# Relative-position buckets of the second block: compared in the expert loop with two bounds, not made ahead by 15 comparisons

## The chip, the cores and the metric

The kernel runs on one core of one Trainium2 chip. The metric is the device time of one execution in microseconds (us), lower is better. Engines are named as in the profile: PE is TensorE, DVE is VectorE, ACT is ScalarE, POOL is GpSimd, SP is the queue engine that issues most DMAs.

## What is computed

Two transformer blocks run one after the other on 256 tokens of width 1024, in float32.

- The first block has an adaptive norm, two attentions of 8 heads each, and a mixture of 32 experts of which each token takes 4.
- The second block has a gated feed-forward, a mixer (a Fourier branch and a differential attention of 4 heads), and a second feed-forward.

The change concerns the bias of the second block's attention. For each query and key the signed distance of their positions picks one of 32 buckets, and the bucket picks a value for each head:

```
rel = positions[key] - positions[query]
bucket = 16 * (rel > 0) + (|rel| if |rel| < 8 else a logarithmic step up to 15)
scores[head, query, key] += rel_bias[bucket, head]
```

The steps of |rel| at which the bucket goes up by one are 15 numbers, `TWO_SIDED = [1, 2, ..., 8, 12, 16, 23, 32, 46, 64, 91]`.

## The kernel before, in words

All of it is one program with hand-written instruction streams for SP, POOL, ACT, PE and DVE that meet at semaphores. On DVE the helper `link` makes an operation count up a semaphore and waits for it at once, so that the next one may read what it wrote.

**Opening and first projection.** SP streams weight slabs of 4 MB into a ring of four slots. In the order of the stream these are two slabs of the adaptive norm, three of `w_in`, one more of the norm, and so on; a slab is loaded once the last user of its slot is done (L573, `release`). Each projection is made of pieces. ACT copies a piece to a high part (`split_until`, L735), DVE subtracts to get the low part (`split_until`, L1622, the operation is L1630), and PE multiplies (L1042 to L1044). `copy_units` on DVE (L1652) makes these low parts and copies results out of PSUM.

**The buckets.** At the very start DVE makes the signed distances of all 256 x 256 pairs (`distances`, L1792) as a tile `REL` of 128 x 512. Then it turns them into buckets: three operations (L1806 to L1808) make the absolute value and the 16 of the positive side, and `buckets` (L1810) adds one comparison per step, each over 128 x 512 elements and each through the helper `stt` (L1618). Six comparisons come before the first norm (L1855), and three stand after each of the first three pairs of projection units (L1857 to L1859). ACT waits for them before the first attention (L891). POOL waits too, and copies the result to the tile `BK` after the attention has used its space (L690, L691).

**The expert loop.** SP loads each expert's 12 MB in six parts of 2 MB (L547). There are nine places for parts, and a part waits until PE has used the one nine before it. PE gathers the tokens of each expert in chunks of 32, multiplies (L1354), turns the gates (L1382), gathers for the next expert (L1336), multiplies down (L1411) and adds into the totals (L1421). DVE runs a loop of 4 passes over 8 unrolled experts (L2038). For each expert e it makes the gates of e (L2012), the row selector (L1790) and the selection (L1947) for e+1, the products of e once PE's gate and up products are there (L2024 to L2034), and the gathered tokens of e+1 (L2006). Last in the body it makes the part of the position bias that belongs to bucket e: a mask `BKM` where the bucket equals e (L2054), and for each of four heads `BIAS2 += BKM * value` (L2057 to L2060, through L1618). So the 32 buckets are spread over the 32 experts.

**After the loop** comes the post-norm of the first block (L1759 on DVE), then the second block. Its attention reads `BIAS2` in two parts (L2089 to L2094).

Of the kernel before, what the change touches and what calls it, by code (L numbers as in the profile page):

```python
# [23 lines left out]
ALU = mybir.AluOpType  # L24
# [3 lines left out]
P = 128  # L28
T = 256
# [6 lines left out]
NE = 32  # L36
# [20 lines left out]
CAUSAL_BUCKETS = [1, 2, 3, 4, 5, 6, 7, 8, 9, 10, 11, 12, 13, 14, 15, 16, 19, 21, 24, 27, 31, 35, 40, 46, 52,  # L57
                  59, 67, 77, 87, 99, 113]

C_ID, C_FLIP, C_MASK, C_TRI, C_OH, C_IOTA, C_END = 0, 128, 256, 384, 896, 1152, 1280  # L60

R_C, R_GPM, R_GPF, R_F1, R_MN, R_F2, R_ADA, R_SUB, R_END = 0, 8, 16, 24, 32, 40, 48, 96, 97

# [1 line left out]
def tables():  # L65

    k = np.zeros((P, C_END), np.float32)
    i = np.arange(P)
    k[:, C_ID:C_ID + P] = i[:, None] == i[None, :]
    k[:, C_FLIP:C_FLIP + P] = i[:, None] == P - 1 - i[None, :]  # L70
    k[:, C_MASK:C_MASK + P] = np.where(i[None, :] > i[:, None], NEG, 0.0)
    t = np.arange(T)
    for tt in range(TT):
        k[:, C_TRI + tt * T:C_TRI + (tt + 1) * T] = (tt * P + i)[:, None] <= t[None, :]
    bucket = np.searchsorted(CAUSAL_BUCKETS, T - 1 - t, side="right")
    k[:NE, C_OH:C_OH + T] = np.arange(NE)[:, None] == bucket[None, :]
    k[:, C_IOTA:C_IOTA + P] = i
    f = np.zeros((P, 5 * T), np.float32)
    for st in range(TT):
        a = 2 * np.pi * ((st * P + i)[:, None] * t[None, :] % T) / T  # L80
        f[:, st * 2 * T:st * 2 * T + T] = np.cos(a)
        f[:, st * 2 * T + T:(st + 1) * 2 * T] = np.sin(a)
    b = 2 * np.pi * (i[:, None] * i[None, :] % P) / P
    f[:, 4 * T:4 * T + P] = np.cos(b) / math.sqrt(T * P)
    f[:, 4 * T + P:5 * T] = -np.sin(b) / math.sqrt(T * P)
    return k, f


def two_blocks(nc, a, const1, const2, out):
    with ExitStack() as ctx:  # L90
        def sb(name, cols, parts=P, dt=F32):
            return ctx.enter_context(nc.sbuf_tensor(name, [parts, cols], dt))
# [27 lines left out]
        HTf, arena = rows_and_arena[:, 0:KT * T], rows_and_arena[:, KT * T:KT * T + ARENA_COLS]  # L120
        HT = HTf.rearrange("p (k t) -> p k t", k=KT)
        K1 = sb("ident", P)
        IOTA = sb("iota", P)
        ONES = sb("ones", P)
        VALS = sb("vals", 32 * 4)
        VC = sb("veccols", 104)
# [86 lines left out]
        NP = T + TT  # L213
        POS_RAW, POS_HI, POS_LO = (HTf[:, 260 * j:260 * j + NP].bitcast(I32) for j in range(3))
        POS_HF, POS_LF = (HTf[:, 780 + 260 * j:780 + 260 * j + NP] for j in range(2))
        REL, BKX = area(13272, TT, T), area(14808, TT, T)
        RTMP = HTf[:, 0:TT * T].rearrange("p (a b) -> p a b", a=TT)

        GS = area(4096, KT, T)
        HH = part("hidden_high", arena_at, 6144, FT * T)[:, :].rearrange("p (k t) -> p k t", k=FT)  # L220
# [415 lines left out]
        def _(pool):  # L636
# [50 lines left out]

            gate_rows(1, 5, "g_post_ffn")
            pool.wait_ge(sem("att_turned"), NHEAD // 2)
            pool.wait_ge(sem("buckets"), 1)  # L690
            link(pool.tensor_copy(BK, BKX))  # L691
            pool.sem_inc(sem("pool_kept"), 1)
            link(pool.memset(BIAS2, 0.0))
            pool.sem_inc(sem("pool_kept"), 1)
# [13 lines left out]
        def _(act):  # L708
# [7 lines left out]
            load(K1[:, :], const1[:, C_ID:C_ID + P], "k_in")  # L716
            load(OH, const1[0:NE, C_OH:C_OH + T], "oh_in")
            load(RB1, a["rel_bias"], "oh_in")
            load(IOTA[:, :], const1[:, C_IOTA:C_IOTA + P], "tri_in")
            load(TRI, const1[:, C_TRI:C_TRI + 2 * T].rearrange("p (t n) -> p t n", t=TT), "tri_in")  # L720

            def f(out_, in_, func=ACT.Copy, **kw):
# [165 lines left out]
                act.wait_ge(sem("att_mixed"), j + 1)  # L888
                f(MIXH[:, j, :], PS[:, MIX_BANK[j], 0:T]).then_inc(sem("mix_high"), 1)

            act.wait_ge(sem("buckets"), 1)  # L891
            split_at = {3: 0, 5: 2, 6: 3}
            for p in range(NHEAD // 2 + 1):
                if p == NHEAD // 2:
# [713 lines left out]
        def _(dve):  # L1608
# [183 lines left out]
            def distances():  # L1792

                dve.wait_ge(sem("pos_in"), 32)
                v.tensor_scalar(POS_HI, POS_RAW, 16, None, ALU.arith_shift_right)
                link(v.tensor_scalar(POS_LO, POS_RAW, 65535, None, ALU.bitwise_and))
                v.tensor_copy(POS_HF, POS_HI)
                link(v.tensor_copy(POS_LF, POS_LO))
                for tt in range(TT):
                    ins = v.tensor_scalar(REL[:, tt, :], POS_HF[:, 0:T], POS_HF[:, T + tt:T + tt + 1], 65536.0,  # L1800
                                          ALU.subtract, ALU.mult)
                link(ins)
                for tt in range(TT):
                    ins = stt(REL[:, tt, :], POS_LF[:, 0:T], POS_LF[:, T + tt:T + tt + 1], REL[:, tt, :], ALU.subtract, ALU.add)
                link(ins)
                link(v.tensor_scalar(BKX, REL, 0.0, 16.0, ALU.is_gt, ALU.mult))  # L1806
                link(v.tensor_scalar(RTMP, BKX, 0.125, -1.0, ALU.mult, ALU.add))
                link(v.tensor_tensor(REL, REL, RTMP, ALU.mult))  # L1808

            def buckets(n0, n1):  # L1810
                for step_at in TWO_SIDED[n0:n1]:
                    link(stt(BKX, REL, float(step_at), BKX, ALU.is_ge, ALU.add))

            def ada_row(part, n):

# [36 lines left out]
            link(v.tensor_scalar(ST[:, 73:74], VC[:, R_SUB:R_SUB + 1], 1.0 - LAMBDA_INIT, None, ALU.mult))  # L1852
            dve.wait_ge(sem("curve_A"), 1)
            v.tensor_tensor(COND[:, :], COND[:, :], VC[:, 0:8], ALU.mult).then_inc(sem("opening_D"), 1)
            buckets(0, 6)  # L1855
            norm(0, AB[:, 8:16], AB[:, 0:8])
            for n in range(3):  # L1857
                copy_units(m0[0] + 2 * n, m0[0] + 2 * n + 2)
                buckets(6 + 3 * n, 9 + 3 * n)  # L1859
            dve.sem_inc(sem("buckets"), 1)  # L1860
            dve.wait_ge(sem("trow_out"), 16)
            v.tensor_copy(ID_R, ident)
            dve.wait_ge(sem("mask_in"), 32)
# [174 lines left out]
            with dve.Fori(0, NE // DVE_TURN) as i:  # L2038
                for q in range(DVE_TURN):
# [10 lines left out]
                    chunks(dve, n_next, e + 1, spread((q + 1) % 2), [sem("xt_sb")])  # L2050

                    dve.wait_ge(sem("pool_kept"), 2)
                    dve.wait_ge(sem("bias2"), e * 2 + 1)
                    v.tensor_scalar(BKM, BK.rearrange("p a b -> p (a b)"), IOTA[:, bass.ds(e, 1)], None,  # L2054
                                    ALU.is_equal).then_inc(sem("bias2"), 1)
                    dve.wait_ge(sem("bias2"), e * 2 + 2)
                    for h in range(4):  # L2057
                        acc = BIAS2[:, h, :, :].rearrange("p a b -> p (a b)")
                        ins = stt(acc, BKM, VALS[:, bass.ds(e * 4 + h, 1)], acc, ALU.mult, ALU.add)
# [147 lines left out]
```

## Time and profile before

| | us |
|---|---|
| median of 3 runs | 1714.8 |
| lowest and highest of them | 1712.97, 1719.04 |
| span of the profiled execution | 1709.8 |
| PE busy in it | 1466.4 (86%) |
| DVE busy in it | 769.3 (45%) |
| ACT busy in it | 463.4 (27%) |
| POOL busy in it | 24.1 (1%) |

The span runs from the first to the last instruction of one profiled execution. The page gives no further time of that execution, so the span is the time of its own that the working is made against; the median of the runs lies 5.0 us above it. The rows are read this way: the number before an engine is a time within the span or a duration in us, what stands in square brackets is how long the engine had been idle just before and what it was waiting for, and "xN" is the number of instructions.

### The profile page before, as it was taken

How to read it: one execution, taken by the hardware profiler on the slowest of the kernel's cores; microseconds unless marked ns; L12 is line 12 of the kernel's file. 1: busy time of each engine (PE TensorE's matmuls, PEld its weight loads, DVE VectorE, ACT ScalarE, POOL GpSimd, SP SyncE). 2: the span in 40 equal slices, each digit the busy share in tenths (PEclk: the TensorE clock that was granted, in tenths of full speed). 3: DMA queues.
4: the chain of work that ended last, by engine and by line, in shares of the span. 5: the costliest groups of instructions: out<-in, count | busy, mean ns of one | idle time of the engine just before them, and what ended most of it. 6: DMA issues, size and time to landing. Idle time of an engine off the chain costs nothing. (4 is left out here: it accounts for less than half of the span.)

```text
span 1709.8 us, 26362 instructions
## 1 busy us (share of the span) xinstructions
PE 1466.4 (86%) x10243; PEld 847.9 (50%) x10243; DVE 769.3 (45%) x1447; ACT 463.4 (27%) x881; POOL 24.1 (1%) x48
## 2 busy tenths in 40 slices
PE   4999888887898999779977665759999999999998
PEld 3977522322232333213322111228888877988887
DVE  4776532332242332323332221337775647767764
ACT  2535310000010010000100000026554537556553
POOL 2002000000000000000000000000000000000000
PEclk9999999999899999889999898889999999999999
DMA  9878799999999999999999999982454742505460
GB/s 349 317 273 334 283 386 424 426 425 424 427 425 427 426 423 405 425 426 426 425 427 425 425 425 426 426 344 102 173 209 194 288 162 90 192 28 197 164 255 25
DMA packets 69011, 549.32 MB, mean 321 GB/s; under 512 B 6001, under 2 KB 6778, under 8 KB 44250
## 3 DMA queue, kind: packets, MB, share of 16 engines
q1 hardware_dynamic: 66392, 542.67, 77.1%
q0 software_dynamic: 1744, 3.53, 0.6%
q8 instruction: 138, 2.26, 0.5%
q10 hardware_dynamic: 690, 0.48, 0.1%
q14 instruction: 47, 0.39, 0.1%
HBM read 545.59 MB, written 1.07 MB: 320 GB/s over the span
## 5 line engine op out<-in xcount | busy, mean ns | idle before, releaser
L1354 PE MATMUL PS<-ring,arena 128*32 128x512 f32 x2768 | 342.4, 633 | 87.1 <-DMA ring<-in_w_gate_up 83.0
L1630 DVE TENSOR_TENSOR weights_low<-ring,weights_high 128x1024 fp32r<-128x1024 f32 x212 | 257.7, 1220 | 86.0 <-ACT weights_high L723 86.0
L1048 PE MATMUL PS<-ht_pair,weights_high 128*128 128x512 f32 x832 | 291.9, 396 | 3.9 <-DVE weights_low L1630 2.6
L2024 DVE TENSOR_SCALAR arena<-PS 128x256 f32<-128x256 f32 x47 | 19.9, 424 | 529.7 <-PE PS L1354 529.7
L723 ACT ACTIVATE weights_high<-ring 128x1024 fp32r<-128x1024 f32 x212 | 222.6, 1056 | 97.1 <-PE PS L1044 97.0
L723 ACT ACTIVATE arena<-PS 128x256 f32<-128x256 f32 (+2 forms) x237 | 100.6, 432 | 516.8 <-PE PS L1411 343.1
L1354 PEld LDWEIGHTS PS<-ring,arena 128*32 128x32 f32 x2768 | 84.4, 113 | 314.8 <-issue 186.3
L1050 PE MATMUL PS<-ht_pair,weights_low 128*128 128x256 f32 x832 | 232.0, 279 | 0.0
L1048 PEld LDWEIGHTS PS<-ht_pair,weights_high 128*128 128x128 f32 x832 | 156.1, 188 | 41.9 <-issue 4.8
L723 ACT ACTIVATE arena<-arena 128x256 f32<-128x256 f32 (+2 forms) x113 | 45.7, 405 | 451.7 <-DVE arena L2024 447.4
L1050 PEld LDWEIGHTS PS<-ht_pair,weights_low 128*128 128x128 f32 x832 | 156.7, 188 | 0.0
L1411 PE MATMUL PS<-ring,arena 128*32 128x512 f32 x1264 | 144.4, 594 | 13.2 <-PEq L492 11.5
L1421 PE MATMUL PS<-arena 64*128 64x512 f32 x384 | 104.3, 673 | 8.6 <-PEq L492 7.9
L1411 PEld LDWEIGHTS PS<-ring,arena 128*32 128x32 f32 x1264 | 44.8, 109 | 112.1 <-issue 106.4
L1618 DVE SCALAR_TENSOR_TENSOR arena<-arena,vals 128x512 f32<-128x512 f32 x128 | 87.7, 748 | 5.9 <-DVE arena L2054 2.1
L1336 PE MATMUL PS<-XN,arena 128*32 128x256 f32 x768 | 57.5, 435 | 21.3 <-ACTq L492 18.6
L1421 PEld LDWEIGHTS PS<-arena 64*128 64x128 f32 x384 | 41.5, 207 | 59.5 <-issue 57.8
L1042 PE MATMUL PS<-weights_high,hidden_high 128*128 128x512 f32 x176 | 68.5, 389 | 0.0
L1044 PE MATMUL PS<-weights_high,hidden_low 128*128 128x512 f32 x176 | 68.5, 389 | 0.0
L1043 PE MATMUL PS<-weights_low,hidden_high 128*128 128x512 f32 x176 | 68.5, 389 | 0.0
L1043 PE MATMUL PS<-ht_pair,weights_high 128*128 128x256 f32 x192 | 54.3, 283 | 0.0
L1667 DVE TENSOR_TENSOR arena<-PS,arena 128x256 f32<-128x256 f32 x60 | 25.4, 424 | 58.0 <-ACT arena L723 57.8
(292 smaller groups left out, 1637.2 us busy)
## 6 DMA issues: line engine op xcount, KB each, us to landing
ring<-in_w_gate_up SPq DMA_DIRECT2D x117, 2048.0 KB, 33.7
ring<-in_w_down SPq DMA_DIRECT2D x54, 2048.0 KB, 35.5
ring<-in_w_ada SPq DMA_DIRECT2D x6, 4096.0 KB, 16.2
ring<-in_w_in SPq DMA_DIRECT2D x6, 4096.0 KB, 13.9
arena<-in_w_gate_up SPq DMA_DIRECT2D x11, 2048.0 KB, 35.4
arena<-in_w_down SPq DMA_DIRECT2D x10, 2048.0 KB, 35.5
ring<-in_ffn_wg SPq DMA_DIRECT2D x4, 4096.0 KB, 13.3
ring<-in_ffn_wu SPq DMA_DIRECT2D x4, 4096.0 KB, 13.6
```

The source lines that it names most:

```text
L723: return nc.scalar.activation(out_, in_, func, **kw)
L1042: mm(out_, lhs[0], rhs[0], start=first, stop=False, **kw)
L1043: mm(out_, lhs[0], rhs[1], start=False, stop=False, **kw)
L1044: return mm(out_, lhs[1], rhs[0], start=False, stop=last, **kw)
L1048: mm(PS[:, bank, :].rearrange("p (a t) -> p a t", a=2), high, HT_PAIR[:, :, k, :], start=first, stop=False, skip_group_check=True)
L1050: return mm(PS[:, bank, 0:T], low, HT_PAIR[:, 0, k, :], start=False, stop=last, skip_group_check=True)
L1336: ins = mm(PS[CH * t:CH * (t + 1), ROW_BANK[c % INL], 0:QC], SEL[:, tt, o:o + CH], XN[:, tt, t * QC:(t + 1) * QC], start=tt == 0, stop=tt ...
L1354: ins = mm(PS[CH * t:CH * (t + 1), c % INL, :].rearrange("p (u n) -> p u n", u=2), XTE[b][c % INL][:, KT // 2 * half + k, :], w[:, k % 2, ...
L1411: ins = mm(PS[CH * g:CH * (g + 1), DOWN_BANK[c % INL], :], HID[c % INL][:, k + j, :], w[:, k % 4 + j, h * HALF:(h + 1) * HALF], start=k == ...
L1421: ins = mm(total(tt, h), SGT[b][c % INL][r, tt * P:(tt + 1) * P], YS[c % INL][r, :], start=False, stop=False, skip_group_check=True)
L1618: return v.scalar_tensor_tensor(out=out_, in0=in0, scalar=scalar, in1=in1, op0=op0, op1=op1)
L1630: v.tensor_tensor(low, w, high, ALU.subtract).then_inc(sem("split_low"), 1)
```

## The change

The opening still makes the signed distances, but nothing of the absolute value, of the 16 for the positive side, or of the 15 comparisons. The signed distances go to the place where the buckets were (offset 14808), and POOL copies them to `BK` at the same point. ACT's wait at L891 is gone. Two small tables, 32 lower bounds and 32 upper bounds, are added to the constant table and come with the `IOTA` load, which grows from 128 to 192 columns. In the expert loop the one comparison with the bucket number becomes two: distance at least the lower bound of bucket e, then distance at most its upper bound, multiplied into the mask.

```diff
-C_ID, C_FLIP, C_MASK, C_TRI, C_OH, C_IOTA, C_END = 0, 128, 256, 384, 896, 1152, 1280
+C_ID, C_FLIP, C_MASK, C_TRI, C_OH, C_IOTA, C_LEAST, C_MOST, C_END = 0, 128, 256, 384, 896, 1152, 1280, 1312, 1344
...
+    edges = [0, *TWO_SIDED, 1e30]
+    for n in range(NE // 2):
+        k[:, C_LEAST + n], k[:, C_MOST + n] = 1 - edges[n + 1], -edges[n]
+        k[:, C_LEAST + NE // 2 + n], k[:, C_MOST + NE // 2 + n] = max(1, edges[n]), edges[n + 1] - 1
...
-        IOTA = sb("iota", P)
+        IOTA = sb("iota", P + 2 * NE)
...
-        REL, BKX = area(13272, TT, T), area(14808, TT, T)
-        RTMP = HTf[:, 0:TT * T].rearrange("p (a b) -> p a b", a=TT)
+        REL = area(14808, TT, T)
...
-            pool.wait_ge(sem("buckets"), 1)
-            link(pool.tensor_copy(BK, BKX))
+            pool.wait_ge(sem("distances"), 1)
+            link(pool.tensor_copy(BK, REL))
...
-            load(IOTA[:, :], const1[:, C_IOTA:C_IOTA + P], "tri_in")
+            load(IOTA[:, :], const1[:, C_IOTA:C_END], "tri_in")
...
-            act.wait_ge(sem("buckets"), 1)
...
-                link(ins)
-                link(v.tensor_scalar(BKX, REL, 0.0, 16.0, ALU.is_gt, ALU.mult))
-                link(v.tensor_scalar(RTMP, BKX, 0.125, -1.0, ALU.mult, ALU.add))
-                link(v.tensor_tensor(REL, REL, RTMP, ALU.mult))
-
-            def buckets(n0, n1):
-                for step_at in TWO_SIDED[n0:n1]:
-                    link(stt(BKX, REL, float(step_at), BKX, ALU.is_ge, ALU.add))
+                ins.then_inc(sem("distances"), 1)
...
-            buckets(0, 6)
             norm(0, AB[:, 8:16], AB[:, 0:8])
-            for n in range(3):
-                copy_units(m0[0] + 2 * n, m0[0] + 2 * n + 2)
-                buckets(6 + 3 * n, 9 + 3 * n)
-            dve.sem_inc(sem("buckets"), 1)
+            copy_units(m0[0], FORGET)
...
-                    dve.wait_ge(sem("bias2"), e * 2 + 1)
-                    v.tensor_scalar(BKM, BK.rearrange("p a b -> p (a b)"), IOTA[:, bass.ds(e, 1)], None,
-                                    ALU.is_equal).then_inc(sem("bias2"), 1)
-                    dve.wait_ge(sem("bias2"), e * 2 + 2)
+                    away = BK.rearrange("p a b -> p (a b)")
+                    dve.wait_ge(sem("bias2"), e * 3 + 1)
+                    v.tensor_scalar(BKM, away, IOTA[:, bass.ds(e + P, 1)], None, ALU.is_ge).then_inc(sem("bias2"), 1)
+                    dve.wait_ge(sem("bias2"), e * 3 + 2)
+                    stt(BKM, away, IOTA[:, bass.ds(e + P + NE, 1)], BKM, ALU.is_le, ALU.mult).then_inc(sem("bias2"), 1)
+                    dve.wait_ge(sem("bias2"), e * 3 + 3)
```

## Rows read from the trace of the kernel before

**Rows 1.** Busy time by engine in the two halves of the expert loop
```profile
223.00:700.00 477.00, 408.82 (x3350) 137.90 (x3346) 154.35 (x354) 39.93 (x85) 0.00 (x0) 0.97 1.00 422
700.00:1138.00 438.00, 318.81 (x2326) 95.86 (x2318) 118.76 (x267) 26.71 (x57) 0.00 (x0) 0.90 1.00 421
```

**Rows 2.** DMA of 223 to 1130 us: GB/s in 40 equal slices
```profile
GB/s 385 428 425 424 426 426 427 423 425 425 427 426 425 426 427 426 426 421 395 418 425 423 425 427 425 426 425 425 426 425 426 425 426 426 425 425 426 426 426 404
```

**Rows 3.** Waits of PE, 230 to 1140 us: total us, times, longest
```profile
PE PS L1354 <- DMA ring<-in_w_gate_up: 83.0, 40, 3.9
...
PE PS L1344 <- DVE expert_rows L1790: 0.7, 1, 0.7
```

**Rows 4.** PE busy, sum over eight windows that cover 43.6 to 113.2 us
```profile
sum 69.60, PE 69.58; mean PE 8.70
```

**Rows 5.** PE groups, 43.5 to 113.2 us: the one with idle time
```profile
L1042 PE MATMUL PS<-ht_high,weights_high 128*128 128x256 f32 x128 | 36.5, 285 | 0.4 <-DVE weights_low L1630 0.4
```

**Rows 6.** DVE groups by shape, 9 to 66 us: busy us, mean ns
```profile
L1618 DVE SCALAR_TENSOR_TENSOR arena<-arena 128x512 f32<-128x512 f32 x15 | 10.3, 690 | 0.4
...
L1808 DVE TENSOR_TENSOR arena<-arena 128x512 f32<-128x512 f32 x1 | 0.7, 693 | 0.0
...
L1806 DVE TENSOR_SCALAR arena<-arena 128x512 f32<-128x512 f32 x1 | 0.4, 429 | 0.0
```

**Rows 7.** DVE timeline, before the first norm: start us, us
```profile
13.86 0.26 DVE L1842 COPY veccols<-PS 128x97 f32<-128x97 f32 x1 [0.21 <-PE PS L1173]
...
16.43 4.32 DVE L1618 SCALAR_TENSOR_TENSOR arena<-arena 128x512 f32<-128x512 f32 x6
21.29 0.15 DVE L1696 TENSOR_SCALAR stats<-stats 128x1 f32<-128x1 f32 x1 [0.54 <-ACT XN L723]
```

**Rows 8.** DVE timeline, in the first projection
```profile
55.74 2.14 DVE L1618 SCALAR_TENSOR_TENSOR arena<-arena 128x512 f32<-128x512 f32 x3
57.91 1.22 DVE L1630 TENSOR_TENSOR weights_low<-ring,weights_high 128x1024 fp32r<-128x1024 f32 x1
...
67.63 2.44 DVE L1630 TENSOR_TENSOR weights_low<-ring,weights_high 128x1024 fp32r<-128x1024 f32 x2 [0.77 <-ACT weights_high L723]
```

**Rows 9.** SP timeline: two loads of the adaptive norm's weights
```profile
59.16 22.36 SPq L582 DMA_DIRECT2D ring<-in_w_ada  x2
```

**Rows 10.** PE timeline: the first products of the first value piece
```profile
67.15 0.40 PE L1042 MATMUL PS<-weights_high,ht_high 128*128 128x512 f32 x1
67.39 0.40 PE L1043 MATMUL PS<-weights_low,ht_high 128*128 128x512 f32 x1
```

**Rows 11.** DVE groups by shape, 222 to 1140 us: busy, mean ns, idle before
```profile
L1618 DVE SCALAR_TENSOR_TENSOR arena<-arena,vals 128x512 f32<-128x512 f32 x128 | 87.7, 748 | 5.9 <-DVE arena L2054 2.1
...
L2012 DVE TENSOR_SCALAR arena<-iota,arena 128x128 f32<-128x128 f32 x90 | 25.8, 343 | 19.4 <-issue 12.9 <-PE PS L1421 4.9 <-PEq L492 1.5
...
L2024 DVE TENSOR_SCALAR arena<-PS 128x256 f32<-128x256 f32 x46 | 19.5, 424 | 521.2 <-PE PS L1354 521.2
...
L2054 DVE TENSOR_SCALAR arena<-arena,iota 128x512 f32<-128x512 f32 x32 | 15.6, 487 | 11.6 <-DVEq L492 11.6
```

**Rows 12.** DVE timeline: the shortest idle time before an expert's first product
```profile
683.94 0.43 DVE L2024 TENSOR_SCALAR arena<-PS 128x256 f32<-128x256 f32 x1 [7.55 <-PE PS L1354]
```

**Rows 13.** Timeline of DVE and PE at the end of the expert loop
```profile
1134.27 0.49 DVE L2054 TENSOR_SCALAR arena<-arena,iota 128x512 f32<-128x512 f32 x1 [0.35 <-DVEq L492]
1134.89 2.74 DVE L1618 SCALAR_TENSOR_TENSOR arena<-arena,vals 128x512 f32<-128x512 f32 x4
...
1143.22 0.69 DVE L1759 TENSOR_TENSOR XN<-PS,arena 128x512 f32<-128x512 f32 x1 [5.59 <-PEq L492]
...
1150.09 2.50 PE L1056 MATMUL PS<-ident 128*128 128x128 f32 x10 [7.08 <-issue]
...
1150.68 0.88 DVE L1708 TENSOR_SCALAR XN<-X,stats 128x512 f32<-128x512 f32 x2
...
1152.39 1.87 PE L1130 MATMUL PS<-ident,XN 128*128 128x128 f32 x8
```

## The prediction

> **What bounds the kernel now.** I read the times by stage first. In the two halves of the expert loop DVE works 154 of 477 us and 119 of 438 us, PE is granted 0.97 and 0.90 of its clock, and the DMA share is 1.00 with 422 and 421 GB/s [rows 1]. The DMA view of the same stretch shows 425 GB/s in nearly every slice [rows 2]. So from 223 to 1138 us, over half of the span, the weight stream sets the time: its end is its start plus its bytes over its rate. PE's waits agree. It waits 83.0 us for gate-up weights, and for a result of DVE it waits once, 0.7 us [rows 3].
>
> The change moves DVE work from the opening into this loop, so the second question is who bounds the opening, where the comparisons are taken away. The PE windows from 43.6 to 113.2 us add up to 69.58 busy of 69.60 us [rows 4], at full clock, and the one group of products with idle time before it has 0.4 us, at the start of the stretch [rows 5]. PE bounds the first projection, and it is never late for want of DVE inside it. Nine of the fifteen comparisons lie in that stretch. The other six lie before the first norm, beside the arrival of X.
>
> **What the change removes.** Fifteen comparisons of 0.690 us are 10.3 us of DVE; of the three operations before them L1806 has 0.429 and L1808 0.693 [rows 6], and L1807, alike to L1806, about the same as it, so together 1.6 us. In all 11.9 us of DVE time. Where each part stood:
>
> - The three operations before the comparisons end before 13.86 us, and there DVE still waits 0.21 us for a transpose of PE [rows 7]. PE had that from a DMA, not from DVE. Worth: nothing.
> - Six comparisons take 4.32 us from 16.43, so 0.72 each from start to start. Behind them stands the mean of the squares, which starts at 21.29 after 0.54 us of waiting for ACT's sum over X [rows 7]. Without them DVE waits 4.9 us in place of 0.54. The cover is the load of X and ACT's squares; if it were gone, this part would give 4.3 us. Worth: nothing.
> - Nine comparisons, three after each of three pairs of units, take 2.14 us a time, 6.4 us in all [rows 8]. Each delays the low part of the next piece. The plainest case: the split at 57.91 starts the moment the comparisons of 55.74 end [rows 8], so it would come up to 2.1 us earlier. PE does not wait for it [rows 4, 5].
> - The tightest cover is at the change to the value units. PE starts the first value piece at 67.15 with 0.24 us a product [rows 10]; a piece has 12 products, so the next is wanted at 67.15 + 12 x 0.23 = 69.9. Its low part is the first of the two splits that start at 67.63 [rows 8], done about 68.85. That is 1.1 us in hand now, and about 3 without the comparisons. Worth: nothing.
> - The split that ends at 59.13 frees the slot into which SP issues the adaptive norm's third slab at 59.16 [rows 8, 9]. That load starts up to 2 us earlier. The next one on SP waits for PE-paced pieces again (the two take 22.36 us to issue [rows 9]), so the expert stream behind it does not start earlier. Worth: nothing, at most 2 us if the whole stream shifted with it.
> - ACT's wait before the attention and POOL's before its copy are long met: the comparisons end near 64 us, and the first attention follows the last product at 113. Nothing.
>
> **What it adds.** Per expert one more two-tensor operation over 128 x 512. The nearest row is the bias sum of the same line, shape and kind of operand (a scalar per partition, picked by a register): 0.748 us [rows 11]. The comparisons of the opening, with a constant as scalar, are the lower bound, 0.690 [rows 6]. To this comes the gap of a linked operation, 0.14 us from the end at 1134.76 to the start at 1134.89 [rows 13], and perhaps register work for one more address and one more wait value: the mask operation has 11.6 us of that over 32, 0.36 each [rows 11]. So 0.83 to 1.25 us an expert; I take 0.89, since the mask's 0.36 follows other waits and the sum that reads VALS through a register has only the gap. The comparison that stays keeps its form and its 0.487 us. Sum: 32 x 0.89 = 28.5 us of DVE (27 to 40). DVE busy goes from 769.3 to 769.3 - 11.9 + 32 x 0.748 = 781.3 us.
>
> What hides it: the bias is the last thing in the body. Behind it on DVE are the gates of the next expert, its row selector and selection (PE wants all three only after the next gate-up products), then the first product of the next expert, which waits for PE. That wait is 521.2 us in all [rows 11], and before the first product of an expert the shortest is 7.55 us [rows 12]. 1.25 us goes into 7.55 six times. Worth in the loop: nothing. ACT and SP wait for nothing that comes after the bias.
>
> The last expert has no next one. Its bias ends at 1134.89 + 2.74 = 1137.63, and DVE then waits until 1143.22, 5.59 us, for PE's last sum [rows 13]. Even if DVE came late there, PE itself is away for 7.08 us and transposes the normed rows at 1152.39, while DVE has the first half of them at 1150.68 + 0.44 = 1151.12 [rows 13], another 1.2 us in hand. Nothing.
>
> The IOTA load grows from 512 to 768 B a row, 32 KB more, at under 10 us, and nothing reads it before the router. The copy on POOL stays as it is. Nothing.
>
> **A rule against the change.** The trace has, before the gates at three of the loop's turns, idle time with no releaser, 12.9 us together, so 4.3 each [rows 11], and PE has 7.08 us of the same kind where it leaves the expert code [rows 13]. DVE too must skip the code of the crowded case there, inside its 5.59 us, and how much of that the skip takes no row shows. The Trainium skill (Runtime: NRT & Kernel Launch, Instruction fetch mechanics) says that a taken branch out of the pages at hand makes the engine fetch before it goes on. By that rule a body that is longer by eight operations with their register work can only add such stalls; the trace agrees that they exist. What it would give is the third rival.
>
> The sum on the path: 0 removed, 0 added. On the profiled span that is 1709.8 us again, and 5.0 us above it, as before, the median: 1714.8.
>
> **The rivals.**
>
> 1. *The opening was bound by DVE after all* (faster). PE's ends are modelled, so small waits could be hidden in "busy". If the nine comparisons were all exposed: 1714.8 - 6.4 = 1708.4; with the six and the three as well, 1714.8 - 12.3 = 1702.5. Against it: 69.58 of 69.60 us, and products that follow each other at an even pace [rows 4, 10]. For it: only that the splits do start at the end of the comparisons [rows 8]. The one way to a real gain is the earlier load, up to 2 us. Chance of over 0.3%: 0.09.
>
> 2. *DVE becomes the bound of the expert loop* (slower). The place is the next expert's gates, which PE wants right after its gate-up products. It decides from the point where the idle time before an expert's first product is under 1 us. Then each expert is 0.89 longer: 1714.8 + 28.5 = 1743.3. Against it: the shortest such idle time is 7.55 us [rows 12], and the DMA stream would swallow delays of PE anyway. For it: nothing but that DVE's part grows. Chance 0.03.
>
> 3. *Longer code costs a fetch where it is not covered* (inside 0.3% or just over). If DVE's 5.59 us at the loop's end were wholly used by its own skip, the added 1.25 and one more stall of 4.3 would show, less the 1.2 us of PE: 1714.8 + 4.4 = 1719.2. A stall inside the loop is covered by 7.55 us. Chance 0.07, of which about half over 0.3%.
>
> 4. *Another cause of slower*, above all the DMA rate, since nearly a whole stage hangs on it: 0.3% of it would be 3 us. Chance of over 0.3%: 0.04.
>
> That the change does not do what it says I see no way for: the four steps are plain operations.
>
> **How the numbers follow.** The forecast is no change, 1714.8, chance 0.77; with the part of rival 3 within the bound, "same" gets 0.80, "faster" 0.09 and "slower" 0.03 + 0.04 + 0.04 = 0.11. A measurement of this kernel can tell about 0.3%, 5.1 us, from no change; the three runs lie 6.1 us apart. The range has the scatter of such a median, some 3 us either side, beyond it the 2 us of the earlier load and most of rival 1's first case below, and rival 3's 4.4 us above: 1709 to 1720. Rival 2 and the full case of rival 1 are left out.
>
> **What would show it.** In the profile after: (a) L1618 over 128 x 512 without VALS in the opening gone, and DVE idle 4.9 us before L1696; (b) PE from 43.6 to 113.2 as full as now, first product within 0.2 us of 43.6; (c) the low part of the second value piece done by 67.5 rather than 68.9; (d) 32 new operations near 0.75 us, the time from the mask's start to the end of the sums 4.25 in place of 3.36 us; (e) DVE's wait before the first product 0.9 us shorter per expert, some 490 us in all, nowhere under 6; (f) DMA at 1.00 and 425 GB/s throughout, PE leaving the loop within 2 us of 1143. I am wrong if the first projection is shorter by microseconds (rival 1), if PE waits for DVE at L1382 or L1336 (rival 2), or if DVE's post-norm starts well after PE's last sum (rival 3).

## The result: 3.9 us slower, and where the time went

| | before | after |
|---|---|---|
| median, us | 1715.53 (20 runs) | 1719.83 (20 runs) |
| lowest to highest | 1711.12 to 1721.48 | 1716.28 to 1724.59 |
| span of the profiled execution | 1709.8 | 1716.7 |
| PE busy / DVE busy in it | 1466.4 / 769.3 | 1467.7 / 781.4 |

The ratio after to before is 1.0023, interval 1.0013 to 1.0033. By it the change costs 3.9 us (2.2 to 5.7); the two medians lie 4.3 us apart. That is less than the 0.3% that the prediction called detectable, but with twenty runs of each it is clear of the scatter. The forecast of no change was wrong. The median of 1719.83 does lie inside the stated range of 1709 to 1720, but only at its edge, and only because the range had been widened for rival 3.

Most of the profile looks like the forecast. First the opening, in the timeline of DVE in the kernel after (start us, duration us, and idle time before with its releaser in brackets):

```profile
15.96 0.17 DVE L1849 TENSOR_TENSOR cond<-cond,veccols 128x8 f32<-128x8 f32 x1
21.40 0.15 DVE L1698 TENSOR_SCALAR stats<-stats 128x1 f32<-128x1 f32 x1 [5.28 <-ACT XN L726]
...
65.73 2.45 DVE L1632 TENSOR_TENSOR weights_low<-ring,weights_high 128x1024 fp32r<-128x1024 f32 x2 [0.77 <-ACT weights_high L726]
```

Without the six comparisons DVE waits 5.28 us for ACT where it waited 0.54, and starts its next step 0.11 us later than before [rows 7]. The first low part of the value units is done at about 66.95 in place of 68.85 [rows 8]. Neither shortens anything: PE's first projection is as full as before.

Then the groups of DVE in the expert loop, with busy us, mean ns and idle time before:

```profile
L1620 DVE SCALAR_TENSOR_TENSOR arena<-arena,vals 128x512 f32<-128x512 f32 x127 | 87.0, 747 | 4.6 <-DVE arena L1620 0.2
L2003 DVE TENSOR_SCALAR arena<-iota,arena 128x128 f32<-128x128 f32 x90 | 25.8, 343 | 14.9 <-issue 12.9 <-PE PS L1423 1.5 <-PEq L495 0.5
L1620 DVE SCALAR_TENSOR_TENSOR arena<-arena,iota 128x512 f32<-128x512 f32 x32 | 24.0, 752 | 4.7 <-DVE arena L2046 1.8
L2015 DVE TENSOR_SCALAR arena<-PS 128x256 f32<-128x256 f32 x47 | 19.9, 424 | 507.7 <-PE PS L1356 507.7
L2046 DVE TENSOR_SCALAR arena<-arena,iota 128x512 f32<-128x512 f32 x32 | 15.6, 486 | 12.6 <-DVEq L495 12.6
L1792 DVE CAST expert_rows<-arena 128x128 fp32r x31 | 7.0, 227 | 19.5 <-DVEq L495 19.5
```

The 32 new operations take 752 ns each. The wait before an expert's first product falls from 521.2 to 507.7 us in all [rows 11] (8.35 of the 507.7 is the first expert's wait, which the row before does not hold), and from the second expert on its shortest at an expert's start is 9.62 us, so DVE is in nobody's way. One row has more than doubled: before the row selector (L1792, L1790 in the kernel before) DVE was idle for 19.5 us in all, where it was 8.6. The chain of waits below shows what that is.

The windows of the opening and the loop (PE, PEld, DVE, ACT, POOL busy us with counts, then granted clock, DMA share, GB/s), kernel after:

```profile
43.60:113.20 69.60, 69.20 (x488) 64.70 (x488) 45.68 (x52) 28.44 (x36) 0.00 (x0) 1.00 0.68 268
113.20:223.00 109.80, 100.82 (x809) 67.36 (x811) 62.68 (x162) 46.74 (x133) 13.48 (x23) 0.95 0.82 318
223.00:700.00 477.00, 408.68 (x3362) 137.76 (x3354) 167.16 (x372) 40.95 (x87) 0.00 (x0) 0.97 0.99 419
700.00:1138.00 438.00, 314.89 (x2280) 92.61 (x2280) 123.09 (x270) 25.92 (x55) 0.00 (x0) 0.88 1.00 423
```

PE fills the first projection as before (it starts it at 44.00 us in place of 43.62; the missing 0.4 us is that start), and DMA runs at the same share as in [rows 1] once the loop is under way. The waits and the loop's end do not look alike, though. PE's waits from 230 to 1140 us, and its timeline where it leaves the loop, kernel after:

```profile
PE PS L1356 <- DMA ring<-in_w_gate_up: 91.0, 43, 4.1
...
PE PS L1346 <- DVE expert_rows L1792: 0.5, 1, 0.5
```

```profile
1149.32 1.99 PE L1423 MATMUL PS<-arena 64*128 64x512 f32 x8 [0.76 <-ACTq L495]
1158.25 2.50 PE L1058 MATMUL PS<-ident 128*128 128x128 f32 x10 [6.94 <-issue]
```

PE waits 91.0 us for gate-up weights where it waited 83.0 [rows 3], still not for DVE, and starts its work behind the loop at 1158.25 against 1150.09 [rows 13]. Of these 8.2 us some belong to this one execution: the granted clock was 0.95 against 0.97 in 113 to 223 us, and 0.64 to 0.80 in 226 to 238 us where it had been 1.00, and the first experts were already some 4 us behind. What grows inside the loop is the rest, and SP's timeline gives it apart from the start. SP issues the loop's 25th part (each of the 32 experts has six) at 268.44 us before and 272.55 after, and the last, the 192nd, at 1098.67 and 1107.06. From the one to the other it is 830.2 us before and 834.5 after: 4.3 us more, as much as between the medians. This time is called the stretch below.

**Where it grows.** Over nearly its whole length the stream keeps its rate. But a weight part of 2 MB is carried by 16 DMA engines, and it can be used when the last of them is done. The landings of each part in the trace give the time from its first engine to its last. Worked out from them, for the kernels before and after (the number is that spread in us; the last part is the last that has landed by 1146 us):

```
            first part of loop   last part of loop
before      1.7                  18.8
after       1.6                  22.5
```

At the end of the loop seven engines are about level, eight lie 12 to 13 us behind those, and one is last by itself: 5.6 us behind the next one before the change, 9.2 us after it. From 420 us on its lag behind the first engine grows in steps of 1.0 us, and each step shows in the first part that lands after a packet of the queue that the profile calls q14, which carries instructions (a part lands about every 5 us). Of the 21 packets from 420 to 1130 us before, 20 are followed by such a step, and of the 25 after, 24. The one without is at 1046 us before and 1054 after, and a packet between 1041 and 1057 us is in every kernel below. The spread does not only grow: at 665 us before and 671 us after, where the stream slackens (one slice of 2.5 us has 229 and 249 GB/s), it falls from 10.1 to 5.2 us and from 10.4 to 6.7. The DMA queues from 223 to 1130 us, before and after:

```profile
q1 hardware_dynamic: 26501, 381.79, 99.4%
q8 instruction: 97, 1.59, 0.7%
q14 instruction: 30, 0.25, 0.1%
```

```profile
q1 hardware_dynamic: 26109, 379.97, 99.0%
q8 instruction: 96, 1.57, 0.7%
q14 instruction: 33, 0.27, 0.1%
```

A packet of q14 is 8 KB. How many instructions that is can be estimated from the runs: in each pass DVE's loop of 736 instructions takes 8 packets, and one of 368 (in an experiment below) takes 5, so 3 packets hold about 368, some 123 each. I count 128 below. Three more packets are fetched in the loop after the change, one for each of DVE's three back edges (a back edge is the jump from the loop's end to its start): each pass behind the first has 7 before and 8 after (without the one near 1050 us). The first back edge, kernel before, then after (DVE timeline):

```profile
412.91 0.74 DVE L1618 SCALAR_TENSOR_TENSOR arena<-arena,vals 128x512 f32<-128x512 f32 x1
417.85 0.60 DVE L2012 TENSOR_SCALAR arena<-iota,arena 128x128 f32<-128x128 f32 x2 [4.19 <-issue]
418.72 0.23 DVE L1790 CAST expert_rows<-arena 128x128 fp32r x1 [0.27 <-DVEq L492]
```

```profile
419.72 0.75 DVE L1620 SCALAR_TENSOR_TENSOR arena<-arena,vals 128x512 f32<-128x512 f32 x1
424.76 0.60 DVE L2003 TENSOR_SCALAR arena<-iota,arena 128x128 f32<-128x128 f32 x2 [4.29 <-issue]
429.25 0.23 DVE L1792 CAST expert_rows<-arena 128x128 fp32r x1 [3.89 <-DVEq L495]
```

Before, DVE stands once for 4.2 us at the turn and the packets come at 415 and 420 us. After, it stands twice, 4.29 and 3.89 us, and they come at 422, 427 and 432. The reason for the third packet I take from the compiled program of DVE. The loop begins at instruction 332 of it before, and at 311 after, since the opening lost 21 instructions net. The body, 720 instructions before and 736 after, then touches one block of 128 more. The traces hold only instructions that were executed, and agree in the differences: 326 of DVE's stand ahead of the loop before and 305 after.

**The theory:** the change costs time neither by DVE's work nor by the opening, but because the loop's code lies differently across the blocks that DVE fetches. Each pass fetches one block more, each block holds up the one DMA engine that carries it by 1 us, and that engine is already the last of every weight part. **Rivals:** the added work in the loop (the work theory), and something in the shortened opening, such as the earlier loads or TensorE's clock (the opening theory).

### The profile page after: what moved, and what is told of

The parts are those of the page before. It is cut to its first block and busy times, and to the rows that moved or that the text cites. A ratio compares the mean times of both kernels' runs of the same rounds, so it can differ in the third digit from the quotient of the medians.

```text
span 1716.7 us, 26404 instructions
## 1 busy us (share of the span) xinstructions
PE 1467.7 (85%) x10243; PEld 848.5 (49%) x10243; DVE 781.4 (46%) x1461; ACT 463.4 (27%) x881; POOL 24.1 (1%) x48
## 5 line engine op out<-in xcount | busy, mean ns | idle before, releaser
L1356 PE MATMUL PS<-ring,arena 128*32 128x512 f32 x2768 | 351.0, 645 | 94.9 <-DMA ring<-in_w_gate_up 91.0
L2015 DVE TENSOR_SCALAR arena<-PS 128x256 f32<-128x256 f32 x47 | 19.9, 424 | 507.7 <-PE PS L1356 507.7
L726 ACT ACTIVATE weights_high<-ring 128x1024 fp32r<-128x1024 f32 x212 | 222.9, 1057 | 99.3 <-PE PS L1046 99.2
L1413 PE MATMUL PS<-ring,arena 128*32 128x512 f32 x1264 | 143.9, 594 | 13.3 <-PEq L495 11.3
L1423 PE MATMUL PS<-arena 64*128 64x512 f32 x384 | 100.8, 659 | 8.6 <-PEq L495 7.7
L1338 PE MATMUL PS<-XN,arena 128*32 128x256 f32 x768 | 53.2, 409 | 21.7 <-ACTq L495 19.1
```

What stands on the lines that cost most here:

```text
L726: return nc.scalar.activation(out_, in_, func, **kw)
L1338: ins = mm(PS[CH * t:CH * (t + 1), ROW_BANK[c % INL], 0:QC], SEL[:, tt, o:o + CH], XN[:, tt, t * QC:(t + 1) * QC], start=tt == 0, stop=tt ...
L1356: ins = mm(PS[CH * t:CH * (t + 1), c % INL, :].rearrange("p (u n) -> p u n", u=2), XTE[b][c % INL][:, KT // 2 * half + k, :], w[:, k % 2, ...
L1413: ins = mm(PS[CH * g:CH * (g + 1), DOWN_BANK[c % INL], :], HID[c % INL][:, k + j, :], w[:, k % 4 + j, h * HALF:(h + 1) * HALF], start=k == ...
L1423: ins = mm(total(tt, h), SGT[b][c % INL][r, tt * P:(tt + 1) * P], YS[c % INL][r, :], start=False, stop=False, skip_group_check=True)
```

## The experiments

In all of them the kernel before ran on the same chip in turn, and ratios are to it. Its median was 1715.74 us beside the opening alone, the loop alone, the loop moved back and the kernel after in one pass; 1716.23 beside the loop moved on, the kernel before in one pass, ACT's loop written out and two experts in a pass in the kernel after; 1715.57 beside two experts in a pass in the kernel before and four in a pass. The ratios are not those of the medians, and can differ from them by 0.1%.

### The opening alone

The new opening with the old loop, body 720 instructions, loop at instruction 311. The first lines show the opening as it differs from the kernel before, the last ones the loop's single comparison, which is kept. It compares the signed distance with the bucket's number, so this kernel leaves out the right position bias, but not its work.

```diff
-            buckets(0, 6)
             norm(0, AB[:, 8:16], AB[:, 0:8])
-            for n in range(3):
-                copy_units(m0[0] + 2 * n, m0[0] + 2 * n + 2)
-                buckets(6 + 3 * n, 9 + 3 * n)
-            dve.sem_inc(sem("buckets"), 1)
+            copy_units(m0[0], FORGET)
...
                     v.tensor_scalar(BKM, BK.rearrange("p a b -> p (a b)"), IOTA[:, bass.ds(e, 1)], None,
                                     ALU.is_equal).then_inc(sem("bias2"), 1)
```

> The changed opening with the loop of before: no absolute value and no 15 comparisons, and one comparison per expert of the signed distance with the bucket number, so the position bias of the second block is not the reference's. Page theory (the DVE loop body begins 23 instructions earlier and so covers one more 8 KB block of instructions in each pass, and these blocks are fetched by the one DMA engine that lands every weight part last): DVE/ACT instruction packets in the loop as in the changed kernel, 33 and not 31, the lag of the last DMA engine at the loop's end near 22 us and not 19, time 3 to 4 us over before. Work theory (the added 0.75 us of DVE per expert costs the 4 us): no added work here, so the time of before, within 1 us. Opening theory (the shorter opening itself makes a later start of the weight stream, by TensorE clock dips): over before by 2 to 4 us, and seen as a later stream already at 235 us.

Measured: 1720.83 us, ratio 1.002 (1.0004 to 1.0036), so 3.4 us over the kernel before (0.7 to 6.2). The loss is there with no new work in the loop. From 223 to 1130 us its q14 row is that of the kernel after, 33 packets, the spread at the loop's end is 22.4 us, and the stretch 834.5. This rules out the work theory; it leaves the opening and the code's place.

### The loop alone

The kernel before with two comparisons in the loop where there was one, both with the bucket's number.

```diff
-                    dve.wait_ge(sem("bias2"), e * 2 + 1)
-                    v.tensor_scalar(BKM, BK.rearrange("p a b -> p (a b)"), IOTA[:, bass.ds(e, 1)], None,
-                                    ALU.is_equal).then_inc(sem("bias2"), 1)
-                    dve.wait_ge(sem("bias2"), e * 2 + 2)
+                    away = BK.rearrange("p a b -> p (a b)")
+                    dve.wait_ge(sem("bias2"), e * 3 + 1)
+                    v.tensor_scalar(BKM, away, IOTA[:, bass.ds(e, 1)], None, ALU.is_ge).then_inc(sem("bias2"), 1)
+                    dve.wait_ge(sem("bias2"), e * 3 + 2)
+                    stt(BKM, away, IOTA[:, bass.ds(e, 1)], BKM, ALU.is_le, ALU.mult).then_inc(sem("bias2"), 1)
+                    dve.wait_ge(sem("bias2"), e * 3 + 3)
```

> The kernel before, with a mask made by two comparisons of the bucket (at least e, at most e): opening untouched, the added DVE operation per expert as in the change. Page theory: the body begins where it began before and is 9 to 18 instructions longer, which by the block count stays within the same blocks, so 31 instruction packets, lag near 19 us, and the time of before within 1 us. Work theory: 3 to 4 us over before. Opening theory: the time of before.

Measured: 1715.43 us, ratio 0.9993 (0.9976 to 1.0009); 30 packets of q14 in the window, spread 18.2 us, stretch 830.6. The 24 us of added DVE work cost nothing (its interval to before allows at most 1.5 us).

### The kernel after, its loop moved back by 24 instructions

```diff
             copy_units(m0[0], FORGET)
+            for _ in range(48):
+                dve.wait_ge(sem("distances"), 1)
```

> The changed kernel with 48 waits that are long met in the opening of DVE (24 instructions), so that its loop begins where it began before, at the same place in its blocks. Page theory: 31 packets in the loop, lag near 19 us, time 3 to 4 us under the changed kernel, so that of before. Work theory and opening theory: the changed kernel's time, 4 us over before.

Measured: 1716.64 us, ratio 0.9996 (0.9978 to 1.0015). Everything of the change is in it, and 24 instructions that do nothing take its loss away (its interval to before still allows 2.6 us). The stretch is 830.9 us, within 0.7 us of the kernel before's. The window has 30 packets, and at its back edges DVE stands once again. The waits of DVE from 223 to 1140 us, then q14:

```profile
DVE arena L2005 <- issue: 13.0, 3, 4.4
DVE arena L2048 <- DVEq L495: 11.1, 28, 0.5
DVE expert_rows L1792 <- DVEq L495: 9.8, 28, 0.7
```

The row selector's 19.5 us, with a longest of 3.9, have become 9.8 with a longest of 0.7. The opening theory falls unless the waits themselves did it, which the next one tells.

### The kernel before, its loop moved on by 70 instructions

```diff
+            for _ in range(140):
+                dve.wait_ge(sem("curve_A"), 1)
             with dve.Fori(0, NE // DVE_TURN) as i:
```

> The kernel before with nothing changed but 140 waits that are already met (70 more DVE instructions) just ahead of the expert loop, so that the loop's code begins 70 instructions later within the program. In the runs so far the instruction queue of DVE and ACT (q14) carried 30 packets in 223:1130 where the loop began at instruction 332 or 335, and 33 where it began at 311; a packet is 8 KB, 128 instructions of 64 bytes. At 402 the loop's 720 instructions again touch one block more. Alignment theory: 33 packets in 223:1130, the last DMA engine's lag at the loop's end about 22 us (it is 18.8 before), the time 3 to 4 us above before, ratio 1.002. Rival (the few met waits of the padded kernel helped by themselves, or the chip's spread made the difference): 30 packets or no change of the time. Opening or removal theory: nothing is removed here, so the time stays at before's.

Measured: 1722.19 us, ratio 1.0032 (1.0018 to 1.0045). Nothing was added to the kernel before but waits that are already met, and it becomes about as slow as the kernel after; the size, 5.5 us with an interval from 3.1 to 7.7, is more than the 3 to 4 expected at its middle. Spread 21.5 us, stretch 835.2, and the queue, 223 to 1130 us:

```profile
q14 instruction: 33, 0.27, 0.1%
```

One thing differs from the kernel after. Its third packet at the turns does not stop DVE a second time: the row selector's wait stays at 8.7 us, longest 0.5. The first stop is a little longer, 14.4 us over the three turns (longest 5.2) where the kernels before and after have 12.9. So the loss does not need DVE's second stop; it goes with the packet.

### No back edge: DVE's loop written out for 32 experts

```diff
-DVE_TURN, ACT_TURN = 8, 8
+DVE_TURN, ACT_TURN = 32, 8
```

In the kernel after:

> The changed kernel with DVE's loop unrolled over all 32 experts, so no back edge and no block fetched twice; the work is the same. Page theory: about 23 instruction blocks of DVE in the loop and not 33 less ACT's own, the lag of the last engine at the loop's end 8 to 12 us and not 22, the stream ends 6 to 10 us earlier, until the next DMA engines are as late; time 5 to 9 us under the changed kernel and under before. Work theory: the changed kernel's time within 1 us, less the three stalls of 4.3 us of DVE if those matter. Opening theory: the changed kernel's time.

Measured: 1713.15 us, ratio 0.9975 (0.996 to 0.999). In the kernel before:

> The kernel before with DVE's expert loop written out for all 32 experts (no back edge). Alignment and fetch theory: about 21 packets on the instruction queue of DVE and ACT in 223:1130 as in the changed kernel in one pass, and the same time as that one (1713.2, ratio 0.9975), since the changed kernel's other differences cost nothing. If the change had a part of its own that pays or costs apart from the fetches, this run would differ from that one by more than 1.5 us.

Measured: 1711.38 us, ratio 0.9966 (0.9949 to 0.9982). Both have 21 packets of q14 in the window, spreads of 14.7 and 14.4 us, and no stop with "issue" at the gates. They differ by 1.8 us, a little over the 1.5 that I had set; their intervals overlap widely, and each has its own runs of the kernel before beside it, so a part of the edit's own of that size is neither shown nor excluded by these times. The stretch shows none inside the loop: 826.0 us in both.

### ACT's loop written out too

```diff
-DVE_TURN, ACT_TURN = 8, 8
+DVE_TURN, ACT_TURN = 32, 32
```

> The changed kernel with DVE's and ACT's expert loops both written out for all 32 experts. If ACT fetches its loop again in each of its four passes, this saves its fetches at the back edges, about 5 packets, and the time falls by up to 5 us under the kernel with DVE alone in one pass (1713.2), to 1708 to 1712. If ACT's loop (some 330 instructions for 8 experts) stays in the engine's buffer and is fetched once, as the 30 packets of before suggest (28 of them are DVE's 7 in each of 4 passes), then writing it out adds 8 to 10 packets, and the time rises by up to that many us, to 1716 to 1722.

Measured: 1711.68 us, ratio 0.9967 (0.9955 to 0.9978). Here the expectation went half wrong. The window has 27 packets, six more than with DVE alone, so by the expectation's reading ACT's loop of 328 instructions was fetched once and then kept, and writing it out costs fetches. But the time did not rise, and the spread at the loop's end is 14.9 us, as with 21 packets. One reason is in the landings: in the kernels with DVE's loop in one pass no engine is alone at the end; the last and the eight next to it lie within 2.5 us (3.2 us here), where in the kernel before the last was 5.6 us behind the next. Another is not excluded: ACT's packets may go by another DMA engine than DVE's. The packet near 1050 us, which is there whatever DVE's loop is and adds no lag even where one engine is last by itself, shows that not every packet of q14 delays that engine.

### Two experts in a pass

```diff
-DVE_TURN, ACT_TURN = 8, 8
+DVE_TURN, ACT_TURN = 2, 8
```

In the kernel after, 184 instructions in the loop, 16 passes:

> The changed kernel with DVE's expert loop of 2 experts in a pass, 16 passes, 184 instructions of code in the loop. If each back edge makes DVE fetch its blocks again, that is 3 to 4 packets in each of 16 passes, 48 to 64 in 223:1130 in place of 33, the last DMA engine lags by 35 us or more, and the time is 15 to 30 us over the changed kernel: 1735 to 1750. If a loop this short stays in the engine's buffer, as ACT's longer one seems to, there are under 10 packets, the lag at the loop's end falls by 10 us or more, and the time falls below the kernel in one pass, to 1700 to 1712. Theory of DVE's work or of the back edges' own time: 15 back edges in place of 3, each under 1 us and beside the weight stream, 1719 to 1720.

Measured: 1711.89 us, ratio 0.9962 (0.9948 to 0.9977). In the kernel before:

> The kernel before with 2 experts in a pass of DVE's loop. Fetch theory: about 5 packets on the instruction queue of DVE and ACT in 223:1130, as in the changed kernel with 2 in a pass, the last DMA engine's lag at the loop's end near 15 us, which is what the other engines' code (TensorE's) leaves, and 1711 to 1713 us, the same as that kernel to 1.5 us. If the edit had a cost or a gain of its own apart from the fetches, the two would differ by more.

Measured: 1711.85 us, ratio 0.9975 (0.9962 to 0.9988). The two medians agree to 0.04 us, closer than these runs can tell: by the two ratios the kernels would lie 2.2 us apart, with intervals that overlap. Inside the loop the stretches say the same, 826.3 and 826.2 us. With the fetches gone, no cost or gain of the edit itself is seen. The queues from 223 to 1130 us and the start of PE's work behind the loop, kernel after with two in a pass:

```profile
q8 instruction: 98, 1.61, 0.7%
q14 instruction: 5, 0.04, 0.0%
```

```profile
1145.21 2.50 PE L1058 MATMUL PS<-ident 128*128 128x128 f32 x10 [6.93 <-issue]
```

Five packets in place of 33; PE leaves at 1145.21 instead of 1158.25 in these two executions. The short loop stays with the engine: fifteen back edges, no stop at the gates. Spreads 15.9 and 16.7 us, not less than with 21 packets. Eight engines now lie level in front and eight together at the end, and the distance grows in steps of about 1.5 us. The other instruction queue, q8, with packets of 16 KB (98 packets, 1.61 MB), is the one left that could do this: there are twelve such steps from 223 to 1145 us, about one for each eight packets. No run here took it away.

### Four experts in a pass

```diff
-DVE_TURN, ACT_TURN = 8, 8
+DVE_TURN, ACT_TURN = 4, 8
```

> The changed kernel with 4 experts in a pass, 8 passes, 368 instructions in the loop, which touch 4 blocks of 128. Fetch theory, if a loop of this length doesn't stay in the engine's buffer: 5 packets in each pass, about 40 in 223:1130 in place of 33, a lag of 27 to 30 us, and 5 to 8 us over the changed kernel, 1725 to 1728. If it stays (184 instructions did): under 10 packets and 1711 to 1713. Theory of the back edges' own time or of DVE's work: 1719 to 1720.

Measured: 1727.28 us, ratio 1.0079 (1.0059 to 1.0099), 7.5 us over the kernel after. The loop of 368 instructions touches four blocks and is not kept. Its queue in the window, DVE's waits from 223 to 1140 us, and PE behind the loop:

```profile
q14 instruction: 41, 0.34, 0.1%
```

```profile
DVE arena L2003 <- issue: 40.8, 10, 4.6
...
DVE expert_rows L1792 <- DVEq L495: 22.8, 27, 3.9
```

```profile
1162.74 2.50 PE L1058 MATMUL PS<-ident 128*128 128x128 f32 x10 [7.04 <-issue]
```

Eight packets more than after, 4.3 us more spread (26.8), the last engine is now 17 us behind the next, and the stretch is 842.6 us, 8.1 more than after. Seven back edges cost this much where fifteen, with two experts in a pass, cost nothing. So it is not the edge, it is what is fetched.

### All together

Packets of q14 in 223 to 1130 us, the spread of the last part before 1146 us, and the stretch (from SP's issue of the 25th part of the loop to that of the last) are from one profiled execution each, the time is the median:

```
kernel                          loop at  body  q14  spread  stretch  median us
before, 2 in a pass                332    180    5    16.7    826.2    1711.85
after, 2 in a pass                 311    184    5    15.9    826.3    1711.89
before, one pass                                21    14.4    826.0    1711.38
after, one pass                                 21    14.7    826.0    1713.15
after, one pass, ACT too                        27    14.9    824.8    1711.68
before, two comparisons            332    728   30    18.2    830.6    1715.43
before                             332    720   30    18.8    830.2    1715.53
after, 24 instructions more        335    736   30    20.3    830.9    1716.64
after                              311    736   33    22.5    834.5    1719.83
new opening, old loop              311    720   33    22.4    834.5    1720.83
before, 70 instructions more       402    720   33    21.5    835.2    1722.19
after, 4 in a pass                 311    368   41    26.8    842.6    1727.28
```

The stretch sorts the kernels by their packets, whatever their work and their opening: 830.2 to 830.9 us with 30, 834.5 to 835.2 with 33, 842.6 with 41. With 5 to 27 it is 824.8 to 826.3, and there it falls no further with fewer packets. Within a group it differs by less than the medians do, since it leaves out when the loop began. The 25th part was issued between 267.9 and 275.1 us in these executions, early and late ones with either opening, so the opening does not show in it.

## Why the prediction was wrong

By its own steps:

- **What bounds the kernel.** Right as to the stage, and wrong in one sentence: "its end is its start plus its bytes over its rate". The rate is a mean over 16 engines, and the end is the last engine's. With 425 GB/s in nearly every slice in both kernels [rows 2], that engine's lag went from 18.8 to 22.5 us. No row that I read showed it, since each gives a mean.
- **The opening.** Right: all three parts of the removed work were hidden, PE full in the first projection, (a) and (c) as forecast (5.28 us of idle time against 4.9). Of (b), the fullness came true, but the first product was at 44.00 us, 0.4 us late where 0.2 was allowed; with the same opening and the old loop it was at 43.70, so that is this execution's own. Rival 1 did not happen.
- **The added work.** Right: 752 ns against 748, DVE busy 781.4 against 781.3, mask to end of the sums 4.27 against 4.25, the shortest wait before an expert's first product 9.62 us. The wait's total was 507.7, not some 490; without the first expert's 8.35 it is 499.4, and a loop that grew by 4.3 us holds more of it. The loop-only kernel shows that this work is free. Rival 2 did not happen.
- **"Worth: nothing" for what was taken away and the step "A stall inside the loop is covered by 7.55 us".** Here it failed. I had seen the three stops of 4.3 us at the turns and took them for what a fetch costs. They are covered, and are still: PE waited for DVE once, 0.5 us. The fetch has a second price, on the DMA engine that carries it, and that one is not covered where the weight stream is the bound. And I looked for more code only in the body. The instructions removed ahead of the loop did it, by moving the loop over a block boundary; a longer body alone did not (728 instructions at 332 and 736 at 335 both have 30 packets). In the sum on the path, "0 removed, 0 added", the missing term is one packet more in each of three passes: 4.3 us of stretch.
- **Rival 3** had the right subject, fetching, with the wrong place (the loop's exit, on DVE's own time), so its 4.4 us agree with the measured 3.9 only by chance. The rule of the Trainium skill (Runtime: NRT & Kernel Launch, Instruction fetch mechanics) on taken branches was to be weighed for its condition too: it speaks only of a branch whose target is outside the pages at hand. The trace agrees, with 5 packets and no stop at two experts in a pass.
- **(f)** failed as it should: rate as forecast, but PE left the loop 8 us later, not within 2 us.

How far this is shown. That the loss goes with the number of packets, and not with the work, is shown: at equal work the loop's place alone made the kernel after faster and the kernel before slower, and the length of a pass moved the time both ways, as expected of the fetches. That the price is paid through the last engine of each weight part rests on the landings: steps of 1.0 us that follow the packets where one engine is last by itself, and a spread that rises with the time as long as one engine is last, and stops falling when others are level with it. The trace does not name the engine of a packet, so this part is inferred. The sizes fit roughly: by the medians three packets cost 4.3 us and eight more 7.5, by the stretch 4.3 and 8.1, which is 1.0 to 1.4 us a packet.

**The faster version.** Two experts in a pass beat both kernels: 1711.89 us with the change and 1711.85 without, against 1719.83 and 1715.53.

## What to carry to other kernels

When a stage is bound by DMA, count the instruction packets in it as well: a hardware loop that no longer fits what its engine keeps is fetched again in every pass, and a packet can delay one DMA engine and with it every transfer that is spread over all of them. Try the number of iterations written out in a loop in both directions, and compare the packets of the instruction queues before comparing times. A change of a few microseconds from an edit that only adds or removes instructions ahead of such a loop should be repeated with the loop's code shifted before it is put down to the work.

## What the runs showed of the hardware

- DVE and ACT fetch code in packets of 8 KB on one queue, q14: with DVE's loop short its packets fell from 33 to 5, and with ACT's written out they rose from 21 to 27. q8 carries instruction packets of 16 KB; for which engine no run tells.
- DVE kept a loop of 180 or 184 instructions over its back edges (5 packets); that ACT kept one of 328 is inferred from the six packets more when it was written out. DVE did not keep one of 368 that touches four blocks (5 packets in each pass). Whether the bound is between 328 and 368 instructions or in the blocks touched was not tried.
- A refetch at a back edge stops DVE for 4.2 to 5.2 us while the weight stream runs. A packet of 8 KB put the last DMA engine back by 1.0 us (24 of 25 packets from 420 us on in the kernel after), three times the 0.3 us that the packet itself is recorded with.
- With two experts in a pass, so nearly without DVE's fetches, the spread of a 2 MB part still grows to 16 us in 900 us, in steps of about 1.5 us, on half of the engines. It falls by several us where the stream slackens.
